# A two-layer hybrid trunk in float32 on one core: another schedule for the second layer's attention

## The reference, cut to what matters

```python
def diff_attend(q, k, v, lam):
    s = jnp.einsum('bqhcd,bkhcd->bchqk', q, k).astype(jnp.float32) * HEAD_DIM ** -0.5
    p = jax.nn.softmax(s, axis=-1)
    a = (p[:, 0] - lam * p[:, 1]).astype(v.dtype)
    return jnp.einsum('bhqk,bkhv->bqhv', a, v)

def finish(o, g):                      # inside diff_attn_layer
    o = rms_norm(o, head_norm) * (1.0 - lambda_init)
    return (o.reshape(g.shape) * jax.nn.silu(g)) @ w_out
```

## Time and profile before

| | |
|---|---|
| median of 3 executions | 1281.92 us (1280.1 to 1285.08) |
| the profiled execution | 1278.96 us |
| its span, first to last instruction | 1277.1 us |
| PE busy | 1182.1 us, 93% |
| DVE, ACT, POOL busy | 618.0, 340.5, 213.8 us |
| mean granted PE clock | 0.985 |
| first scores of step 0 | 864.27 us |
| last matmul block begins | 1245.57 us |

### The profile page before, as it was taken

One profiled execution on the slowest core, in us unless ns is written; L12 is line 12 of the kernel. 1 busy time (PEld: TensorE's weight loads), 2 busy tenths in 40 slices (PEclk: granted clock), 3 DMA queues, 4 the chain that ended last, 5 costly groups with the idle time before them and its releaser, 6 DMA issues.

```text
span 1277.1 us, 12416 instructions
## 1 busy us (share of the span) xinstructions
PE 1182.1 (93%) x4543; PEld 635.0 (50%) x4543; DVE 618.0 (48%) x1218; ACT 340.5 (27%) x746; POOL 213.8 (17%) x198
## 2 busy tenths in 40 slices
PE   3699999999999999999999999999999998878878
PEld 0455667565555444555544444444455444445543
DVE  0466662367786646666601235403454633435553
ACT  1411113112222234544400121103233323324430
POOL 2200000657662310000000004200121300000000
PEclk9899999999999999999999999999999999899999
DMA  9701102014434111001003041201011100100001
GB/s 312 269 1 37 66 27 105 1 64 160 174 132 171 52 50 50 1 1 50 1 1 115 1 144 46 86 0 66 26 42 66 66 34 16 51 1 1 1 1 66
DMA packets 40466, 81.50 MB, mean 64 GB/s; under 512 B 2470, under 2 KB 3975, under 8 KB 40407
## 3 DMA queue, kind: packets, MB, share of 16 engines
q1 hardware_dynamic: 36165, 68.83, 15.3%
q10 hardware_dynamic: 3122, 8.57, 1.9%
q0 software_dynamic: 1120, 3.32, 1.0%
HBM read 78.58 MB, written 2.13 MB: 63 GB/s over the span
## 4 chain that ended last, share of the span: by engine, by line
PE 87%; DVE 4%; ACT 3%; DMA 3%; issue 2%; POOL 1%; SPq 1%; DVEq 0%; ACTq 0%
PE ps L656 43%; PE ps L905 9%; PE ps L833 6%; PE ps L941 4%; PE ps L786 3%; PE ps L815 3%; PE ps L963 3%; PE ps L802 2%; PE ps L953 2%; PE ps L852 2%; PE ps L695 2%; PE ps L884 2%; PE ps L874 2%; DMA ring<-in_mod_w_dram 1%; ACT xs_all L1618 1%
## 5 line engine op out<-in xcount | busy, mean ns | idle before, releaser
L656 PE MATMUL ps<-ring,hT 128*128 128x512 f32 (+1 forms) x832 | 348.9, 577 | 1.0 <-DVE hT L1078 1.0
L656 PEld LDWEIGHTS ps<-ring,hT 128*128 128x128 f32 x832 | 158.0, 193 | 173.6 <-issue 167.4
L656 PE MATMUL ps<-hT,ring 128*128 128x256 f32 (+1 forms) x512 | 169.2, 487 | 3.5 <-DVE pool_mem L1094 2.0
L1663 POOL TENSOR_SCALAR stat<-stat 128x8 f32<-128x8 f32 (+3 forms) x52 | 22.8, 438 | 761.9 <-DVE stat L1240 258.0
L656 PEld LDWEIGHTS ps<-hT,ring 128*128 128x128 f32 x512 | 96.1, 190 | 73.2 <-issue 65.8
L1272 DVE TENSOR_REDUCE stat<-ps 128x1 f32<-128x768 f32 x64 | 60.9, 952 | 65.1 <-PE ps L941 65.1
L833 PE MATMUL ps<-ring,hT 128*128 128x512 f32 x192 | 88.9, 594 | 0.8 <-DVE pool_mem L1295 0.8
L905 PE MATMUL ps<-ring,hT 128*128 128x512 f32 x192 | 85.7, 593 | 1.8 <-DMA ring<-in_ev_w_out_dram 1.8
L1337 DVE TENSOR_TENSOR pool_mem<-ps,pool_mem 128x512 f32<-128x512 f32 x28 | 19.3, 690 | 112.9 <-PE ps L905 87.2
L1664 POOL TENSOR_TENSOR stat<-stat 128x8 f32<-128x8 f32 (+3 forms) x52 | 67.4, 1296 | 4.3
L1719 POOL TENSOR_TENSOR pool_mem<-consts,dtv 128x512 f32<-128x512 f32 x48 | 57.2, 1199 | 37.0 <-PE ps L786 37.0
(11 more groups left out here) (180 smaller groups left out, 1431.5 us busy)
## 6 DMA issues: line engine op xcount, KB each, us to landing
ring<-in_mod_w_dram SPq DMA_DIRECT2D x11, 2048.0 KB, 9.0
ring<-in_od_w_in_dram SPq DMA_DIRECT2D x8, 2048.0 KB, 7.8
ring<-in_ev_w_in_dram SPq DMA_DIRECT2D x7, 2048.0 KB, 8.2
ring<-in_ev_w_out_dram SPq DMA_DIRECT2D x4, 1536.0 KB, 6.6
ring<-in_od_w_out_dram SPq DMA_DIRECT2D x2, 2048.0 KB, 7.8
ring<-in_mod_w_dram ACTq DMA_DIRECT2D x1, 2048.0 KB, 15.1
xs_all<-in_x_dram POOLq DMA_DIRECT2D x4, 512.0 KB, 9.1
xs_all<-in_x_dram ACTq DMA_DIRECT2D x4, 512.0 KB, 5.6
```

What stands on the lines that cost most here:

```text
L656: mm = pe.matmul(bank[:, 0:width], lhs_of(k), rhs_of(k), start=(k == 0), stop=(k == count - 1))
```

## The change

Three things are changed, all in the second layer.

1. The turns have two buffers: `qT1` and `kT1` become lists of two, for even and odd heads. The second ones lie in tiles that the first layer has done with (`consts` behind the identity, and a new tile `dcd` that holds the former `decay`, `cdec` and `dtv`). The three turns of head h + 1 are spread over steps 0, 1 and 2 of head h, behind the scores. `otr` gets a fixed step (11, 13, 15, 19, 23, 27, 31), and `hnorm` of a head comes one step after its last `pv1`.
2. The output projection is in three parts: `out1a` over heads 0 to 3 (four matmuls a unit), `out1b` over heads 4 and 5 (two a unit), and `out1` over heads 6 and 7 (two a unit). All of `out1a` and the first half of `out1b` are fills, and every step has a fill.
3. In a step `exp1` stands ahead of `ptr1`, so ACT issues the two exponentials before the copy of the transposes.

```diff
--- before.py
+++ after.py
@@ -176,46 +176,36 @@
     fill = [("g1", 0, 0)] + [u for t in range(1, 4) for u in (("g1", 0, t), ("k1", 1, t - 1))]
     fill += [("k1", 1, t) for t in range(3, NT)]
     fill += [("q1", 1, t) for t in range(NX)] + [("v1", 1, t) for t in range(NT)]
-    gate_fill = [("g1", 1, t) for t in range(NX)]
-    early_out = [("out1a", n, t) for n in range(2) for t in range(NX)]
+    fill += [("g1", 1, t) for t in range(NX)] + [("out1a", n, t) for n in range(2) for t in range(NX)]
+    fill += [("out1b", n, t) for n in range(2) for t in range(NX)]
     work = [(h, t) for h in range(C_HEADS) for t in range(NX)]
-    late, ropes = [], []
+    out_turn = {11: 0, 13: 1, 15: 2, 19: 3, 23: 4, 27: 5, 31: 6}
+    ropes = []
     st += [("hk", 0, 1), ("hq", 0), ("hk", 0, 0)]
-    for n in range(len(work) + 1):
-        if n < len(work):
-            st += [("sc1",) + work[n] + (c,) for c in range(2)]
+    for n in range(len(work)):
+        h, t = work[n]
+        st += [("sc1", h, t, c) for c in range(2)]
+        if h < C_HEADS - 1 and t < 3:
+            st.append((("hk", h + 1, 1), ("hq", h + 1), ("hk", h + 1, 0))[t])
+        if n in out_turn:
+            st.append(("otr", out_turn[n]))
+        st.append(("exp1", h, t))
         if n >= 1:
             st.append(("ptr1",) + work[n - 1])
-        if n < len(work):
-            h, t = work[n]
-            st.append(("exp1", h, t))
-            if t == NX - 1 and h < C_HEADS - 1:
-                st += [("hk", h + 1, 1), ("hq", h + 1), ("hk", h + 1, 0)]
-                if h + 1 == 3:
-                    st.append(("gates", 1))
-            st += ropes
-            ropes = []
-            st.append(("comb1", h, t))
-        now = []
-        if n < 16:
-            now = [fill.pop(0) for _ in range(1 + (n in (1, 2, 3, 9)))]
-        elif n < 20:
-            now = [gate_fill.pop(0)]
-        elif early_out and n % 3 != 2:
-            now = [early_out.pop(0)] if len(early_out) > 2 else []
+        if n == 10:
+            st.append(("gates", 1))
+        st += ropes + [("comb1", h, t)]
+        now = [fill.pop(0) for _ in range(1 + (n in (1, 2, 3, 9, 31)))]
         st += now
-        ropes += [("rope",) + u for u in now if u[0] in ("k1", "q1")]
+        ropes = [("rope",) + u for u in now if u[0] in ("k1", "q1")]
         if n >= 1:
             st.append(("pv1",) + work[n - 1])
-            if work[n - 1][1] == NX - 1:
-                late += [("hnorm", work[n - 1][0]), ("otr", work[n - 1][0])]
         if n == 16:
             st.append(("gatesum", 1))
-        if n >= 12 and n < len(work):
-            for _ in range(2):
-                if late:
-                    st.append(late.pop(0))
-    st += late[:1] + early_out + late[1:]
+        if n >= 5 and n % 4 == 1:
+            st.append(("hnorm", n // 4 - 1))
+    st += [("ptr1",) + work[-1], fill.pop(0), ("pv1",) + work[-1], ("hnorm", C_HEADS - 1)] + fill
+    st.append(("otr", C_HEADS - 1))
     st += [("out1", n, t) for n in range(2) for t in range(NX)]
     return st
 
...
@@ -383,10 +373,10 @@
         qkw = bc[:, 0:256]
         sink, dtb, alog, dskip = bc[:, 256:264], bc[:, 264:296], bc[:, 296:328], bc[:, 328:344]
         nsink, lam = bc[:, 344:352], bc[:, 352:356]
-        dtv = sb("dtv", 2 * 192)
+        dcd = sb("dcd", 960)
+        decay, cdec, dtv = dcd[:, 0:384], dcd[:, 384:576], dcd[:, 576:960]
         dt_v, dta_v = dtv[:, 0:192], dtv[:, 192:384]
-        decay = sb("decay", 384)
-        cdec = sb("cdec", 192)
+        o_junk = sb("o_junk", C_V)
         stat = sb("stat", 192)
 
         ident, le, ge, gt, lt = (consts[:, n * P:(n + 1) * P] for n in range(5))
...
@@ -444,8 +434,8 @@
         oT = [carve(first + j * SEQ, SEQ) for first, count in ((6144, 4), (D, 2), (8192, 2)) for j in range(count)]
         g1v = carve(10240, NX * D).rearrange("p (t n) -> p t n", t=NX)
         L1 = 14336
-        qT1 = carve(L1, SEQ)
-        kT1 = carve(L1 + 1024, TOK)
+        qT1 = [carve(L1, SEQ), consts[:, P:5 * P]]
+        kT1 = [carve(L1 + 1024, TOK), dcd[:, 0:TOK]]
         probT1 = carve(L1 + 1792, 768).rearrange("p (b t) -> p b t", b=NT)
         sq1 = [carve(L1 + 2560, 512), carve(L1 + 512, 512)]
         rope_a1, rope_b1 = carve(L1 + 3072, 512), carve(L1 + 3584, 512)
...
@@ -938,7 +928,7 @@
                     for lo, hi in ((0, 512), (512, TOK)):
                         for comp in range(2):
                             half = slice(comp * HD, (comp + 1) * HD)
-                            mm = pe.matmul(pair(n + comp)[:, lo:hi], qT1[half, t * P:(t + 1) * P], kT1[half, lo:hi],
+                            mm = pe.matmul(pair(n + comp)[:, lo:hi], qT1[h % 2][half, t * P:(t + 1) * P], kT1[h % 2][half, lo:hi],
                                            start=True, stop=True)
                             if hi == TOK:
                                 mm.then_inc(sc_ready, 1)
...
@@ -966,15 +956,15 @@
                 elif kind == "otr":
                     pe.wait_ge(o_ready, a[0] + 1)
                     turn(stage, [g1v[:, t, a[0] * P:(a[0] + 1) * P] for t in range(NX)])
-                elif kind in ("out1a", "out1"):
-
-                    first = 0 if kind == "out1a" else C_HEADS // 2
+                elif kind in ("out1a", "out1b", "out1"):
+
+                    first, count = {"out1a": (0, 4), "out1b": (4, 2), "out1": (6, 2)}[kind]
                     if a == (0, 0):
-                        for h in range(first, first + C_HEADS // 2):
+                        for h in range(first, first + count):
                             wait_done(pe, ("otr", h))
                     (w,) = slabs(stage)
                     project(stage, SLAB, lambda k: oT[first + k][:, a[1] * P:(a[1] + 1) * P],
-                            lambda k: w[:, first + k, :], C_HEADS // 2)
+                            lambda k: w[:, first + k, :], count)
 
 
         @block.vector
...
@@ -1330,8 +1320,10 @@
                         tmp, gate = res_tmp[:, u % 2, :], gate_bc[:, 0 if t < NX else 1, n * SLAB:(n + 1) * SLAB]
                     else:
                         tmp, gate = res_tmp1[:, u % 2, :], gate_bc1[:, n * SLAB:(n + 1) * SLAB]
+                    if stage == ("out1b", 0, 0):
+                        dve.wait_ge(early_ready, 2 * NX)
                     if stage == ("out1", 0, 0):
-                        dve.wait_ge(early_ready, 2 * NX)
+                        dve.wait_ge(middle_ready, 2 * NX)
                     if u >= 2:
                         dve.wait_ge(told, u - 1)
                     V.tensor_tensor(tmp, bank_of(stage), gate, ALU.mult).then_inc(done_sem(stage), 1)
...
@@ -1593,14 +1585,14 @@
                     wait_unit(act, stage)
                     bank = bank_of(stage)
                     if kind == "hq":
-                        if h >= 1:
-                            act.wait_ge(sc_ready, SC1[("sc1", h - 1, NX - 1, 1)] + 1)
-                        A.copy(qT1, bank).then_inc(done_sem(stage), 1)
+                        if h >= 2:
+                            act.wait_ge(sc_ready, SC1[("sc1", h - 2, NX - 1, 1)] + 1)
+                        A.copy(qT1[h % 2], bank).then_inc(done_sem(stage), 1)
                     else:
                         lo, hi = ((0, SEQ), (SEQ, TOK))[a[1]]
-                        if h >= 1:
-                            act.wait_ge(sc_ready, SC1[("sc1", h - 1, NX - 1, 1)] + 1)
-                        A.copy(kT1[:, lo:hi], bank[:, 0:hi - lo]).then_inc(done_sem(stage), 1)
+                        if h >= 2:
+                            act.wait_ge(sc_ready, SC1[("sc1", h - 2, NX - 1, 1)] + 1)
+                        A.copy(kT1[h % 2][:, lo:hi], bank[:, 0:hi - lo]).then_inc(done_sem(stage), 1)
                 elif kind == "v1":
                     if a == (0, 0):
                         act.wait_ge(lam_ready, 1)
...
@@ -1629,7 +1621,7 @@
                     if at(*stage) > 1:
                         act.wait_ge(o_sq, at(*stage) - 1)
                     r = 2 * (at(*stage) - 1) % 8
-                    A.activation(le, bank_of(stage)[:, 0:P], ACT.Square, scale=rinv[:, r:r + 1],
+                    A.activation(o_junk, bank_of(stage)[:, 0:P], ACT.Square, scale=rinv[:, r:r + 1],
                                  accum_out=ss_o[:, h * NX + t:h * NX + t + 1]).then_inc(o_sq, 1)
                 elif kind == "otr":
                     h = a[0]
```

12 lines of the change are left out of this document (6 added, 6 removed).

## The result

The changed kernel takes 1226.58 us (median of 3, 1224.81 to 1227.47) against 1281.92 us; the ratio is 0.956, 95% interval 0.953 to 0.960. It is faster, as forecast, but by 55.3 us and not by 47, and the time lies 1.4 us under the range of 1228 to 1246. The profiled execution took 1226.58 us, its span is 1224.7.

A forecast was written before the change was run, and what follows sets the result against it. PE was taken as the bound, with idle time and slow clock in layer 1's attention. Non-work falling from 58.2 to 10.4 us saves 47.8, taken as 47: median 1281.92 to 1235 us, range 1228 to 1246.

The forecast's parts named there:

- the late copy: Steps 28 to 30: PE waits at `pv1` for the copy behind the exponentials, 1.9 us each, 5.9 in total.
- the near misses: Steps 20 to 27, four matmuls of fill: the copy stays hidden, with 0.3 us in total allowed for PE barely waiting.
- the clock here: Attention of layer 1 after the change: slow clock costs nothing to 5 us, taken as 2.5, for one or two drops.
- the step from the trace to the median below: Whole kernel: the saving of 47 us from the profiled 1278.96 us is applied to the median 1281.92, giving 1235 us.
- Some 15 are slow clock: Attention before the change: of 58.2 us that are no work, 43.4 are idle and some 15 slow clock.
- for what such a sum forgets: Whole sum: the computed saving of 47.8 us is taken as 47 to allow for forgotten costs.
- The clock that takes it back: Rival, steps 20 to 31: short waits keep the clock swinging, costing 10 us instead of 2.5; 1244 us, 12%.
- the late copy in all small steps: Rival, steps 20 to 27: turn copies delay the exponentials, each step waits 1 to 2 us; 1247 us, 7%.
- the banks: Rival, the 28 turns: each waits 0.7 us for a bank that a copy must free; 1255 us, 4%.
- the slower case: Rival, steps with rotations: lateness of the DVE and POOL chain passes from step to step; 1290 us, 2%.
- the one of no effect: Rival, whole kernel: the waits were only moved and PE waits as long elsewhere; 1282 us, 2%.
- The better case: Rival, attention of layer 1: no clock drops, and waits of 1.5 instead of 1.9 us; 1229 us, 7%.

The follow-up runs named there:

- Eleven waits of at most 1.5 us: Changed kernel with ACT held up by three extra copies ahead of the `ptr1` copy in steps 20 to 27: 1238.01 us, ratio 0.966.
- the eleven of 2.5 to 2.8 us: Changed kernel with five extra ACT copies in steps 20 to 27 and two in steps 28 to 30: 1257.34 us, ratio 0.981.
- the third part alone: Kernel before the change with only `exp1` put ahead of `ptr1`: 1301.97 us, ratio 1.016.
- 18.7 us of added waits: Changed kernel with one buffer for the turns of k and q again, output turn of head 0 in step 12: 1256.31 us, ratio 0.981.

## Why the prediction was right or wrong

**Right: what bounds the kernel and which waits go.** Of the waits in the earlier trace rows those for the head's copy, for `hnorm` and for `ptr1` in steps without a fill are gone and the late combination's is 0.2 us; each part undone brought its own back. The terms for the turns (16.6), for `hnorm` (16.9) and for the steps without a fill were right, no turn waits for a bank, and the full steps are 10.50 us long.

**Right with a size off: the late copy.** It was to cost 1.9 us in each of steps 28 to 30, 5.9 in all; it is listed as 1.48 each, 4.4. The copy starts 0.2 us earlier than I had it, half of it by my slip in the sum, and the list counts from the modelled end of the fill; from start to start, as the 1.9 was worked out, PE loses 5.56 - 3.92 = 1.6 us. `hnorm` ahead of step 30 delays nothing: the row maxima start 1.59 us behind the scores (1184.20 behind 1182.61), as in step 29. Of the other small waits, the one for step 10's combination is 0.15 instead of 0.3, the near misses of 0.3 do not exist, the bank in step 31 costs 0.5 instead of 0.3 and the last block 0.8 instead of 1.1. Waits in all: 5.9 instead of 7.9.

**Wrong beside it: what the copy's place could earn.** The prediction said that with the old order these steps "would wait for nothing". Undone, it gave 2.0 us and not the whole of the waits, because DVE's chain came next.

**The steps that failed: the clock here, and the step from the trace to the median below.** "Nothing to 5 us; I take 2.5, for one or two drops" was a guess between ends. The clock is 1.00 throughout, so the term is 0, and of the terms of the sum it is the one that was furthest off. Waits of 1.5 us brought no slow stretch here, eleven of them neither; waits of 2.3 to 3.7 us did at many places. The nearest row was the one at 0.99, and I moved away from it. The Trainium skill ("TensorE: Matmul & The Clock Gate", "A second HAM failure mode: psum-queue depth-cycling") says that frequent short idle times between groups of matmuls can make the clock swing between its levels. Eleven waits of at most 1.5 us, with the clock at 1.00, do not bear it out for waits as short as these; the eleven of 2.5 to 2.8 us, five of which brought slow clock, do in part.

Before the change the term was not quite right either. "Some 15 are slow clock" was what the sum left over. By the granted clock, the attention before has seven slow stretches that cost 1.7 us each, one of them twice that, 13.7 us in all. The rest goes with its waits, which cost a little more than is listed.

**The sum, term by term.** Between the two traces the attention up to the last matmul became 409.0 - 355.1 = 53.9 us shorter. The prediction's sum was 47.8. The difference is 2.0 in the waits, 2.5 in the clock, and 1.6 in the useful work, which I had at 323.1 us: the changed trace gives 341.13 - 5.9 - 13.75 = 321.5. Four transposes take 0.49 us and not 0.56; my row for them lay at the beginning of a slow stretch. The 0.8 us "for what such a sum forgets" went the wrong way. The first scores begin 1.45 us later in the changed trace, so the span shrank by 52.4. Part of that is there at PE's first matmul already (16.67 against 16.03 us), which waits for a transfer; in the traces of the other kernels the first scores begin at 864.07 to 867.36 us.

**And the median.** I moved the saving from the profiled execution (1278.96) to the median (1281.92) unchanged. That is where 3 of the 8.4 us come from, the largest single part. The others are the 2.5 of the clock, the 2.0 of the waits, the 1.6 of the work and the 0.8 for the forgotten, less the 1.45 us of the later start. The executions of the kernel before differ by their clock: of nine in one group, those at a mean clock of 0.985 took 1278.6 and 1278.8 us, those at 0.980 or 0.981 took 1284.4 to 1285.2. The profiled one was at 0.985. The changed kernel has four runs within 0.7 us (1225.31 to 1226.05), though its first three spread over 2.7 (1224.81 at 0.996, 1227.47 at 0.994). So what spread the times of the kernel before goes for the most part with the slow clock that the change takes away, and the median had more to gain than the trace. Taken from the median, the low end of the range would have been 3 us lower, 1225, and the measured time inside.

**The rivals.** The clock that takes it back, the late copy in all small steps, the banks, the slower case and the one of no effect did not come. The better case did, no clock drop and waits of 1.5 us. It had 7%, and its 1229 us was still too high; by its own terms (2.5 of clock and 3 x 0.4 of waits off 1235) it would have been 1231. The slower case had a grain: the third part alone makes the kernel before 1.6% slower, but by the late copy and slow clock and not by DVE's and POOL's chain.

## What to carry to other kernels

A wait of the matrix engine is worth more than its listed length, above all when it is long enough to bring slow clock: here 18.7 us of added waits, nearly all at head changes, cost 30, and 10.6 us of short ones cost 12.7. When one wait is taken away from a short step, look at the in-order engine next to it before giving the gain: moving one copy gave 2 us, moving it with DVE's fill work 6. And when the runs of a kernel spread with their clock, take the saving from the median's clock and not from the one profiled execution.
